# Two-layer hybrid decoder on one core: sparse attention heads on two row halves of TensorE, the fifth step's state-space block behind the value products, compression on two column groups

## The chip, the cores and the metric

One core of one Trainium2 chip runs the whole program. The metric is the device time in microseconds (us) of one execution; the kernel before was timed in three runs. TensorE (PE) multiplies, and its weight loads have rows of their own (PEld); VectorE (DVE), ScalarE (ACT) and GpSimd (POOL) do the rest, and SyncE (SP) issues most transfers. Matmul results land in PSUM, here eight banks of 128 x 512 float32.

## The reference, cut to what matters

```python
for l in range(DEPTH):                              # DEPTH = 2, 256 tokens, width 1024
    u = rms_norm(h_res, norm_mix[l]) @ w_in[l]
    y_a = mla_mixer(u...)      # 4 heads, 64+32 wide, causal softmax attention
    y_b = nsa_mixer(u...)      # 4 heads, 64 wide, three branches over shared keys
    y_c = rglru_mixer(u...)    # gated linear recurrence
    y_d = ssd_mixer(u...)      # state-space block, chunks of 128
    h_res = h_res + concat(rms_norm(y_a), rms_norm(y_b), rms_norm(y_c), y_d) @ w_out[l]
    h_res = h_res + (swiglu if l == 0 else moe_ffn)(rms_norm(h_res, norm_ffn[l]))

def nsa_mixer(u, ...):
    # q: 4 heads x 64; keys and values: 3 pairs x 64, shared by the heads
    kc, vc = compress(keys0), compress(vals0)       # 32 x 64 inputs -> 64, for 15 windows of 32 tokens
    o = gate0 * softmax(q kc) vc + gate1 * softmax(q k_sel) v_sel + gate2 * softmax(q k_win) v_win
```

With 256 tokens the selection takes all four blocks of 64 and the window of 512 covers everything, so "sel" and "win" are both plain causal attention with 64-wide heads.

## The kernel before

Everything is written out by hand: each engine has its own program, and counting semaphores tie them together. There are two layers. In each, a mixer (about 90 us) is followed by a feed-forward part, dense after the first mixer and eight experts after the second, in which w_hi/w_lo parts of the weights are multiplied. All of the change lies in the mixers.

The attention part of a mixer is a pipeline of eight jobs, `AJ = mla0, mla1, sel0, sel1, win0, win1, cmp0, cmp1`: a branch and a block of 128 query tokens (0 or 1). Block 0 sees 128 keys and block 1 sees 256; "cmp" sees 15 compressed keys. At step n the engines do, each in the order of its program:

- TensorE: `scores(n)` (four heads, L732), at n = 4 the state-space block `ssd_sums` (L817 to L838), `products(n - 2)` (probabilities times values, L780), `turn_probs(n - 1)` (transposes of the probabilities, L749); and at n = 0 the gates of the recurrence (L812), at n = 2 inside `products(0)` the compression (`compress`, L790), at n = 3 `turn_keys`, at n = 5 `ssd_cb` (L848), at n = 6 `ssd_products`. `keep_busy` (L713) issues matmuls whose result nobody reads.
- VectorE: `score_rows(n)` (mask, scale and row minimum of each head, L2149), at n = 4 the state-space block (L2218 to L2235), at n = 2 the copy of the compressed keys and values (L2240) and a convolution (`conv`, L2087 and L2091), then `outputs(n - 2)` (L2166 to L2190).
- ScalarE: `exps(n)` (L1576 and L1573), then `turned_probs(n - 1)` (copies the transposed probabilities out of PSUM, L1586), and at n = 2 the two Silu calls (L1630 and L1631) between which and the exponentials it reloads its function table; at n = 4 the exponentials of the state-space block (L1637).

TensorE's results for VectorE go to banks 0 to 3 in turn (`bank(0)`), those for ScalarE to banks 4 to 7 (`bank(1)`); `bank` waits until the bank of four uses ago has been read, and `give` signals that a bank is full. `score_rows(n)` waits until ScalarE has copied out the transposed probabilities of job n - 2, since it writes over that job's `prob`; `products(n)` waits for the copy of job n itself.

A 64-wide float32 head occupies rows (partitions) 0 to 63 of its operands, so half of the array's rows. Each float32 matmul shows as two records in the trace, each with a weight load; a transpose shows as one. Before the pipeline the queries are turned by L679 (64 wide, two heads to a bank, two banks, read by ScalarE's L1552), the compression's inputs by L687 and L688, the keys by L693, and the dense-attention queries and keys by L704 (read by L1563).

Of the kernel before, what the change touches and what calls it, by code (L numbers as in the profile page):

```python
# [22 lines left out]
P = 128  # L23
# [17 lines left out]
def trunk(nc, x, positions, norm_mix, w_in, mla_q_norm, mla_w_uq, mla_kv_norm, mla_w_ukv, nsa_cmp_pe,  # L41
# [33 lines left out]
    with ctx:  # L75
# [101 lines left out]
        def at(start, *shape):  # L177
            used[0] = start
            return take(*shape)

        mix_bufs = []
        for l in range(L):
            i0 = (BASE_MIX[l] + 7) % SPLIT
            b1, b2 = (split_at + SLOT * i for i in (i0, SPLIT + i0))
            b3, b4, b5, b6 = (split_at + SLOT * (SPLIT * j + (i0 + i) % SPLIT) for j in range(2) for i in (1, 2))
            mix_bufs.append((
                at(b1, TB, MLA_H, QK), take(TB, MLA_H, QK),
                at(b2, 2, S), take(6, S),
                at(b3, MLA_H, S), take(MLA_H, S),
                at(b4, NH, S), take(2, S), take(NC), take(2 * HD), take(TB, SSD_H), take(4, HD),  # L190
                at(b5, CLEN // 2, 2, NC), take(TB, GW), take(TB, GW), take(SSD_H, P), at(used[0] - SSD_H * P, 2, S),
                at(b6, SSD_H, S)))
# [18 lines left out]
        def probT_cmp(n):  # L211

            return probT[:, n % 2, 7 * P:8 * P] if n == 6 else probT[:, n % 2, 0:P]

        def prob_of(n):
# [88 lines left out]
        left_hi = sem("left_hi")  # L304
        left_lo = sem("left_lo")
        cn_ready = sem("cn_ready")
        qk_roped, nsa_roped, cin_ready, gate_th = sem("qk_roped"), sem("nsa_roped"), sem("cin_ready"), sem("gate_th")
# [92 lines left out]
        def _(pe):  # L400
# [168 lines left out]
            for l in range(L):  # L569
# [102 lines left out]

                pe.wait_ge(nsa_roped, l + 1)
                for hp in range(2):
                    b = bank(1)
                    for i in range(2):
                        c0 = O_NSA + (2 * hp + i) * HD
                        for tb in range(TB):
                            mm = pe.transpose(b[0:HD, (2 * i + tb) * P:(2 * i + tb + 1) * P],  # L679
                                              utok[:, tb, c0:c0 + HD], ident[:, :])  # L680
                    give(mm, 1)
                b = bank(1)
# [32 lines left out]
                def scores(n):  # L715
                    br, tb = AJ[n]
                    t0, t1 = tb * P, (tb + 1) * P
                    nk = NC if br == "cmp" else t1
                    if br == "cmp":
                        pe.wait_ge(dve_took, mark["cmp", l])  # L720
                    per = 4 if br == "cmp" else 512 // nk
                    for g in range(4 // per):
                        b = bank(0)
                        if n == 7:
                            keep_busy(b, 2)
                        for i in range(per):
                            h = g * per + i
                            q, k = {"mla": (qT[0:QK, h, t0:t1], kT[0:QK, h, 0:nk]),
                                    "cmp": (nqT[0:HD, h, t0:t1], kcT[0:HD, :]),
                                    "sel": (nqT[0:HD, h, t0:t1], kswT[0:HD, 0, 0:nk]),  # L730
                                    "win": (nqT[0:HD, h, t0:t1], kswT[0:HD, 1, 0:nk])}[br]
                            mm = pe.matmul(b[:, i * nk:(i + 1) * nk], q, k, start=True, stop=True)  # L732
                        give(mm, 0)
                    mark["scores", l, n] = gave[0]
# [50 lines left out]
                def compress(b):  # L785

                    pe.wait_ge(cin_ready, l + 1)
                    for c in range(2):
                        for j in range(CLEN // 2):
                            mm = pe.matmul(b[0:NC, c * HD:(c + 1) * HD], cin[:, j, c, :], w_cmp[:, j, c * HD:(c + 1) * HD],  # L790
                                           start=(j == 0), stop=(j == CLEN // 2 - 1))
                    give(mm, 0)
                    mark["ckv", l] = given[0]
# [131 lines left out]
                for n in range(len(AJ) + 2):  # L925
                    if n < len(AJ):
                        scores(n)
                    if n == 4:
                        ssd_sums()
                    if n >= 2:  # L930
# [3 lines left out]
                    if 1 <= n <= len(AJ):  # L934
                        turn_probs(n - 1)
                    if n == 0:
                        lru_gates()
# [269 lines left out]
        def _(pool):  # L1207
# [63 lines left out]

            for l in range(L):
                roots(1, 0, False)
                roots(1, 1)
# [22 lines left out]
                pool.wait_ge(*filled_by[1][mark["nsa", l] - 1])  # L1297
                pool.memset(utok[:, :, KV0 + 4 * HD:KV0 + 4 * HD + 1], 1.0).then_inc(sum_cols, 1)
                roots(2, 0, False)
                roots(2, 2)  # L1300
# [50 lines left out]
        def _(act):  # L1351
# [127 lines left out]
            for l in range(L):  # L1479
# [69 lines left out]

                for hp in range(2):  # L1550
                    b = filled()
                    act.activation(nqT[0:HD, 2 * hp:2 * hp + 2, :],  # L1552
                                   b[0:HD, :].rearrange("p (h t) -> p h t", h=2), ACT.Copy).then_inc(act_took, 1)
                b = filled()
# [213 lines left out]
        def _(dve):  # L1768
# [203 lines left out]
            for l in range(L):  # L1972
# [163 lines left out]
                def score_rows(n):  # L2136
# [3 lines left out]
                    if n >= 2:  # L2140
                        dve.wait_ge(act_took, mark["probT", l, n - 2])
                    per = 4 if br == "cmp" else 512 // nk
                    scale = float(QK if br == "mla" else HD) ** -0.5
                    m = cmbias[:, tb, :] if br == "cmp" else cbias[:, P - tb * P:2 * P]
                    for g in range(4 // per):
                        b = filled()
                        for i in range(per):
                            h = g * per + i
                            ins = dve.tensor_tensor_reduce(prob_of(n)[:, h, :], b[:, i * nk:(i + 1) * nk], m,  # L2149
                                                           -scale, -NEG, ALU.add, ALU.min, rmin[:, n, h:h + 1])  # L2150
                        empty_bank(ins)
# [57 lines left out]
                for n in range(len(AJ) + 2):  # L2209
# [3 lines left out]
                    if n < len(AJ):  # L2213
                        score_rows(n)
                    if n == 4:

# [17 lines left out]
                        for tb in range(TB):  # L2234
                            step(dve.tensor_tensor(xdt[:, tb, :].rearrange("p (h d) -> p h d", h=SSD_H),  # L2235
                                                   xtok[:, tb, :].rearrange("p (h d) -> p h d", h=SSD_H),
                                                   dts[:, 4, tb, :].unsqueeze(2).broadcast_to([P, SSD_H, HD]), ALU.mult))
                    if n == 2:
                        b = filled()
                        empty_bank(dve.tensor_copy(ckv[0:NC, :], b[0:NC, 0:2 * HD]))  # L2240
                        tell(conv(xbc, xraw, "scw", "scb", 6, 4, 6), "ssd_conv", ssd_conv)
                    if 1 <= n <= len(AJ) and AJ[n - 1][0] == "cmp":
                        mask_cmp(n - 1)
                    if n >= 2 and n != 8:
                        outputs(n - 2)

                    if n == 0:
# [406 lines left out]
```

## Time and profile before

| | us |
|---|---|
| Median of 3 runs (1509.17 to 1509.39) | 1509.21 |
| The profiled execution, its own time | 1509.64 |
| Its span in the trace | 1507.9 |
| Attention pipeline of layer 0, first scores to first output projection | 80.6 to 122.5 |
| The same of layer 1 | 457.8 to 499.8 |

Busy time counts the time in which an engine has an instruction in flight. TensorE's matmuls overlap and their ends are modelled, so for TensorE the starts are read: the distance between the starts of two groups is what the first took. The idle time before a group stands in square brackets with what ended it. The second layer's mixer repeats the first's nearly to the hundredth, 377.2 us later.

### The profile page before, as it was taken

What the parts mean: (1) busy time and instruction counts of PE and PEld (TensorE: products, weight loads), DVE (VectorE), ACT (ScalarE), POOL (GpSimd) and SP (SyncE); (2) the same over time, 40 slices, a digit from 0 to 9 for tenths busy, and PEclk for the clock granted to TensorE, in tenths of its full rate; (3) what the DMA queues carried; (4) which work ended last, traced back from release to release, by engine and by line L of the source; (5) the groups of instructions that cost most, each with busy time, mean ns of one, the idle gap of its engine ahead of it and who ended that gap; (6) DMA issues with size and microseconds to landing.
All of it is one profiled execution on the core that took longest, in us unless ns stands there. A gap on an engine that the chain in (4) does not pass through costs nothing.

```text
span 1507.9 us, 20053 instructions
## 1 busy us (share of the span) xinstructions
PE 1486.9 (99%) x7413; PEld 1245.8 (83%) x7413; DVE 1213.4 (80%) x1283; ACT 1000.3 (66%) x894; POOL 82.7 (5%) x126
## 2 busy tenths in 40 slices
PE   9999999999999999999999999999999999999997
PEld 7987888888898888888888888888888888888885
DVE  7778545545577899989898899898988899889986
ACT  7376543444547577787777777777777777778765
POOL 3102000000000110000000000000000000000000
PEclk9999999999999999999999999999999999999999
DMA  9705655555530379999999999999999999999992
GB/s 319 249 2 131 240 176 195 194 195 170 190 115 2 112 274 396 396 354 394 395 346 394 394 356 384 394 380 357 396 394 345 394 396 342 395 396 344 393 396 87
DMA packets 189980, 444.23 MB, mean 295 GB/s; under 512 B 9729, under 2 KB 16014, under 8 KB 189918
## 3 DMA queue, kind: packets, MB, share of 16 engines
q1 hardware_dynamic: 185366, 427.81, 77.5%
q0 software_dynamic: 4528, 15.58, 3.9%
q8 instruction: 39, 0.64, 0.2%
q14 instruction: 23, 0.19, 0.0%
q10 hardware_dynamic: 24, 0.01, 0.0%
HBM read 435.51 MB, written 7.86 MB: 294 GB/s over the span
## 4 chain that ended last, share of the span: by engine, by line
PE 94%; DVE 2%; ACT 2%; issue 1%; POOL 0%; SPq 0%; DMA 0%; POOLq 0%; DVEq 0%; ACTq 0%
PE bank L478 27%; PE bank L479 27%; PE bank L477 27%; PE bank L618 3%; PE bank L540 2%; PE bank L732 1%; PE bank L621 1%; PE bank L780 1%; PE bank L749 1%; PE bank L790 0%; PE bank L1020 0%; DMA ring<-in_w_in_dram 0%; POOL rstd L1303 0%; PE bank L650 0%; PE bank L713 0%
## 5 line engine op out<-in xcount | busy, mean ns | idle before, releaser
L1909 DVE TENSOR_TENSOR w_lo<-ring,w_hi 128x2048 fp32r<-128x2048 f32 x372 | 846.4, 2290 | 176.1 <-ACT w_hi L1427 175.6
L1427 ACT ACTIVATE w_hi<-ring 128x2048 fp32r<-128x2048 f32 x372 | 712.2, 1917 | 221.7 <-PE bank L477 221.7
L478 PE MATMUL bank<-w_hi,xT_hi 128*128 128x512 f32 x896 | 353.5, 395 | 0.0
L479 PE MATMUL bank<-w_hi,xT_lo 128*128 128x512 f32 x896 | 349.4, 390 | 0.0
L477 PE MATMUL bank<-w_lo,xT_hi 128*128 128x512 f32 x896 | 240.2, 390 | 0.0
L478 PE MATMUL bank<-w_hi,hidT_hi 128*128 128x512 f32 x560 | 220.6, 394 | 0.0
L479 PE MATMUL bank<-w_hi,hidT_lo 128*128 128x512 f32 x560 | 218.2, 390 | 0.0
L477 PEld LDWEIGHTS bank<-w_lo,xT_hi 128*128 128x128 f32 x896 | 168.1, 188 | 36.0 <-DVE w_lo L1909 0.3
L479 PEld LDWEIGHTS bank<-w_hi,xT_lo 128*128 128x128 f32 x896 | 168.3, 188 | 33.9
L478 PEld LDWEIGHTS bank<-w_hi,xT_hi 128*128 128x128 f32 x896 | 168.3, 188 | 33.6
L478 PE MATMUL bank<-w_hi,hT_hi 128*128 128x512 f32 (+2 forms) x384 | 147.3, 387 | 4.8 <-DVE hT_lo L1864 2.7
L477 PE MATMUL bank<-w_lo,hidT_hi 128*128 128x512 f32 x560 | 149.4, 389 | 0.0
L479 PE MATMUL bank<-w_hi,hT_lo 128*128 128x512 f32 (+2 forms) x384 | 145.2, 381 | 0.0
L477 PEld LDWEIGHTS bank<-w_lo,hidT_hi 128*128 128x128 f32 x560 | 105.1, 188 | 22.2
L479 PEld LDWEIGHTS bank<-w_hi,hidT_lo 128*128 128x128 f32 x560 | 105.2, 188 | 21.2
L478 PEld LDWEIGHTS bank<-w_hi,hidT_hi 128*128 128x128 f32 x560 | 105.2, 188 | 21.2
L1433 ACT ACTIVATE hidT_hi<-bank 128x512 fp32r<-128x512 f32 x68 | 40.1, 599 | 92.5 <-PE bank L540 92.5
L1887 DVE TENSOR_TENSOR w_lo<-ring,w_hi 128x2048 fp32r<-128x2048 f32 (+1 forms) x34 | 77.1, 2280 | 24.6 <-ACT w_hi L1392 23.2
L477 PE MATMUL bank<-w_lo,hT_hi 128*128 128x512 f32 (+2 forms) x384 | 92.6, 381 | 0.5 <-DVE w_lo L1887 0.5
L478 PEld LDWEIGHTS bank<-w_hi,hT_hi 128*128 128x128 f32 x384 | 72.6, 189 | 20.3 <-issue 3.1
L479 PEld LDWEIGHTS bank<-w_hi,hT_lo 128*128 128x128 f32 x384 | 72.5, 189 | 13.1
L1392 ACT ACTIVATE w_hi<-ring 128x2048 fp32r<-128x2048 f32 (+1 forms) x33 | 62.5, 1904 | 30.9 <-PE bank L477 15.3
(393 smaller groups left out, 1269.6 us busy)
## 6 DMA issues: line engine op xcount, KB each, us to landing
ring<-in_moe_w_gate_dram SPq DMA_DIRECT2D x112, 1024.0 KB, 9.4
ring<-in_moe_w_up_dram SPq DMA_DIRECT2D x112, 1024.0 KB, 9.4
ring<-in_moe_w_down_dram SPq DMA_DIRECT2D x112, 1024.0 KB, 9.1
ring<-in_ffn_w_gate_dram SPq DMA_DIRECT2D x14, 1024.0 KB, 5.2
ring<-in_ffn_w_up_dram SPq DMA_DIRECT2D x14, 1024.0 KB, 5.1
ring<-in_ffn_w_down_dram SPq DMA_DIRECT2D x14, 1024.0 KB, 4.8
ring<-in_w_in_dram SPq DMA_DIRECT2D x11, 1024.0 KB, 5.3
ring<-in_w_out_dram SPq DMA_DIRECT2D x8, 1024.0 KB, 8.9
```

The costliest lines, as they stand in the source:

```text
L477: return pe.matmul(o, x_hi, w, start=False, stop=stop)
L478: pe.matmul(o, x_hi, w, start=start, stop=False)
L479: return pe.matmul(o, x_lo, w, start=False, stop=False)
L540: mm = pe.transpose(banks[2 + v][:, f * P:(f + 1) * P], hid[:, v, f * P:(f + 1) * P], ident[:, :])
L618: mm = pe.matmul(b[i][:, 0:S], wk, hT_hi[:, 4 * h + k, :], start=start and not low, stop=stop and low)
L621: pe.matmul(b[i][:, 0:S], wk, hT_lo[:, 4 * h + k, :], start=False, stop=False)
L732: mm = pe.matmul(b[:, i * nk:(i + 1) * nk], q, k, start=True, stop=True)
L1392: act.activation(dst[:, :, 0:n], slot_k(p)[:, :, 0:n], ACT.Copy).then_inc(hi_ready, 1)
L1427: act.activation(w_hi[:, (base + at) % SPLIT, :], ring[:, i, :], ACT.Copy).then_inc(hi_ready, 1)
L1433: act.activation(hidT_hi[:, v, :], banks[2 + v][:, :], ACT.Copy).then_inc(hidT_hi_ready, 1)
L1887: dve.tensor_tensor(dst[:, :, 0:n], slot_k(p)[:, :, 0:n], hi[:, :, 0:n], ALU.subtract)\
L1909: dve.tensor_tensor(w_lo[:, v, :], ring[:, (base + at) % RING, :], w_hi[:, v, :].bitcast(F32), ALU.subtract).then_inc(lo_ready, 1)
```

## The change

The queries' four 64-wide heads are turned two at a time, so that heads 0 and 2 lie in partitions 0 to 63 and heads 1 and 3 in 64 to 127. GpSimd copies the keys (`kswT`, 64 x 512 float32) and later the compressed keys (`kcT`) to the upper partitions with two transfers per layer. The scores of sel, win and cmp alternate between the two row halves, each half with its own bank; so block 0 now takes two banks where it took one. The dense attention (mla) gets the same interleaving of two banks in block 1, without row halves. The compression alternates between its two operands, the second one's output at partitions 32 to 46. The state-space block of step 4 moves behind `products` and `turn_probs` on TensorE, and behind `outputs` on VectorE.

```diff
-                at(b4, NH, S), take(2, S), take(NC), ...
+                at(b4, NH // 2, S), take(2, S), take(NC), ...
+        def heads_of(n):
+            br, tb = AJ[n]
+            if br == "mla":
+                return [[0, 1, 2, 3]] if tb == 0 else [[0, 1], [2, 3]]
+            return [[0, 2], [1, 3]]
...
                 pe.wait_ge(nsa_roped, l + 1)
+                b = bank(1)
                 for hp in range(2):
-                    b = bank(1)
-                    for i in range(2):
-                        c0 = O_NSA + (2 * hp + i) * HD
-                        for tb in range(TB):
-                            mm = pe.transpose(b[0:HD, (2 * i + tb) * P:(2 * i + tb + 1) * P],
-                                              utok[:, tb, c0:c0 + HD], ident[:, :])
-                    give(mm, 1)
+                    c0 = O_NSA + 2 * hp * HD
+                    for tb in range(TB):
+                        mm = pe.transpose(b[:, (2 * hp + tb) * P:(2 * hp + tb + 1) * P],
+                                          utok[:, tb, c0:c0 + 2 * HD], ident[:, :])
+                give(mm, 1)
...
                     if br == "cmp":
                         pe.wait_ge(dve_took, mark["cmp", l])
-                    per = 4 if br == "cmp" else 512 // nk
-                    for g in range(4 // per):
-                        b = bank(0)
-                        if n == 7:
-                            keep_busy(b, 2)
-                        for i in range(per):
-                            h = g * per + i
-                            q, k = {"mla": (qT[0:QK, h, t0:t1], kT[0:QK, h, 0:nk]),
-                                    "cmp": (nqT[0:HD, h, t0:t1], kcT[0:HD, :]),
-                                    "sel": (nqT[0:HD, h, t0:t1], kswT[0:HD, 0, 0:nk]),
-                                    "win": (nqT[0:HD, h, t0:t1], kswT[0:HD, 1, 0:nk])}[br]
+                        pe.wait_ge(keys_in, 32 * (l + 1))
+                    elif br == "sel":
+                        pe.wait_ge(keys_in, 32 * l + 16)
+                    groups = heads_of(n)
+                    held = [bank(0) for _ in groups]
+                    if n == 7:
+                        keep_busy(held[0], 2)
+                    for i in range(len(groups[0])):
+                        for b, heads in zip(held, groups):
+                            h = heads[i]
+                            r = slice(h % 2 * HD, (h % 2 + 1) * HD)
+                            nq = nqT[r, h // 2, t0:t1]
+                            q, k = {"mla": (qT[0:QK, h, t0:t1], kT[0:QK, h, 0:nk]), "cmp": (nq, kcT[r, :]),
+                                    "sel": (nq, kswT[r, 0, 0:nk]), "win": (nq, kswT[r, 1, 0:nk])}[br]
                             mm = pe.matmul(b[:, i * nk:(i + 1) * nk], q, k, start=True, stop=True)
-                        give(mm, 0)
+                            if i == len(heads) - 1:
+                                give(mm, 0)
...
-                    for c in range(2):
-                        for j in range(CLEN // 2):
-                            mm = pe.matmul(b[0:NC, c * HD:(c + 1) * HD], cin[:, j, c, :], w_cmp[:, j, c * HD:(c + 1) * HD],
-                                           start=(j == 0), stop=(j == CLEN // 2 - 1))
+                    for j in range(CLEN // 2):
+                        for c in range(2):
+                            mm = pe.matmul(b[32 * c:32 * c + NC, c * HD:(c + 1) * HD], cin[:, j, c, :],
+                                           w_cmp[:, j, c * HD:(c + 1) * HD], start=(j == 0), stop=(j == CLEN // 2 - 1))
...
                         scores(n)
-                    if n == 4:
-                        ssd_sums()
                     if n >= 2:
                         products(n - 2)
...
                         turn_probs(n - 1)
+                    if n == 4:
+                        ssd_sums()
...
+                pool.wait_ge(act_took, mark["nsa", l])
+                pool.dma_start(kswT[HD:P, :, :], kswT[0:HD, :, :]).then_inc(keys_in, 16)
+                pool.wait_ge(dve_took, mark["cmp", l])
+                pool.dma_start(kcT[HD:P, :], kcT[0:HD, :]).then_inc(keys_in, 16)
                 roots(2, 0, False)
...
-                for hp in range(2):
-                    b = filled()
-                    act.activation(nqT[0:HD, 2 * hp:2 * hp + 2, :],
-                                   b[0:HD, :].rearrange("p (h t) -> p h t", h=2), ACT.Copy).then_inc(act_took, 1)
+                b = filled()
+                act.activation(nqT[:, :, :], b[:, :].rearrange("p (h t) -> p h t", h=2), ACT.Copy)\
+                    .then_inc(act_took, 1)
...
+                    if n == 2:
+                        b = filled()
+                        dve.tensor_copy(ckv[0:NC, 0:HD], b[0:NC, 0:HD])
+                        empty_bank(dve.tensor_copy(ckv[0:NC, HD:2 * HD], b[32:32 + NC, HD:2 * HD]))
+                        tell(conv(xbc, xraw, "scw", "scb", 6, 4, 6), "ssd_conv", ssd_conv)
+                    if 1 <= n <= len(AJ) and AJ[n - 1][0] == "cmp":
+                        mask_cmp(n - 1)
+                    if n >= 2 and n != 8:
+                        outputs(n - 2)
                     if n == 4:
...
```

VectorE's `score_rows` follows the new grouping of heads; its step-2 copy, `mask_cmp` and `outputs`, which stood behind the block of step 4, now stand ahead of it, and nothing else of them changes but the second copy.

## Rows read from the trace of the kernel before

**Rows 1.** The page, busy time, share of the span and instructions.

```profile
PE 1486.9 (99%) x7413; PEld 1245.8 (83%) x7413; DVE 1213.4 (80%) x1283; ACT 1000.3 (66%) x894; POOL 82.7 (5%) x126
```

**Rows 2.** Timeline of TensorE, layer 0: start, duration, line, shapes, count, [idle before].

```profile
80.58 1.16 PE L732 MATMUL bank<-work 96*128 96x128 f32 x8 [0.86 <-ACT work L1563]
...
83.31 1.89 PE L732 MATMUL bank<-work 96*128 96x256 f32 x8
...
85.57 1.16 PE L732 MATMUL bank<-work 64*128 64x128 f32 x8
86.65 3.75 PE L790 MATMUL bank<-w_cmp,work 128*15 128x64 f32 x64
...
92.24 1.99 PE L732 MATMUL bank<-work 64*128 64x256 f32 x8
...
98.02 0.66 PE L823 MATMUL bank<-ident,work 128*128 128x128 f32 x4
...
101.07 0.49 PE L836 MATMUL bank<-upper,work 128*128 128x128 f32 x2 [0.39 <-DVE work L2149]
...
102.51 1.00 PE L780 MATMUL bank<-work 128*128 128x65 f32 x8
...
104.32 1.99 PE L732 MATMUL bank<-work 64*128 64x256 f32 x8
...
109.92 1.06 PE L732 MATMUL bank<-work 64*128 64x15 f32 x8
```

**Rows 3.** Timeline of TensorE, layer 1.

```profile
478.29 0.49 PE L836 MATMUL bank<-upper,work 128*128 128x128 f32 x2 [0.38 <-DVE work L2149]
```

**Rows 4.** Timeline of ScalarE, layer 0.

```profile
86.05 1.71 ACT L1576 ACTIVATE work<-work 128x256 f32<-128x256 f32 x4 [0.58 <-DVE work L2149]
...
91.91 1.08 ACT L1586 ACTIVATE work<-bank 128x512 f32<-128x512 f32 x2 [0.95 <-PE bank L749]
93.02 1.28 ACT L1630 ACT_TABLE_LOAD   x1
...
97.63 1.71 ACT L1576 ACTIVATE work<-work 128x256 f32<-128x256 f32 x4
99.24 0.57 ACT L1586 ACTIVATE work<-bank 128x512 f32<-128x512 f32 x1
...
105.98 1.04 ACT L1637 ACTIVATE work<-work 128x1024 f32<-128x1024 f32 x1
```

**Rows 5.** Timeline of VectorE, layer 0.

```profile
84.50 0.42 DVE L2149 CUSTOM_DVE_ANT_0 work<-bank,cbias 128x256 f32<-128x256 f32 x1
...
90.44 0.28 DVE L2240 COPY work<-bank 15x128 f32<-15x128 f32 x1 [1.24 <-PE bank L790]
...
104.33 0.75 DVE L2235 TENSOR_TENSOR work<-work 128x256 f32<-128x256 f32 x2
...
119.40 0.18 DVE L2166 RECIPROCAL work<-bank 128x4 f32<-128x4 f32 x1 [1.07 <-PE bank L780]
```

**Rows 6.** Timeline of TensorE, where outputs change partitions (L687 and L688).

```profile
74.13 1.03 PE L679 MATMUL bank<-ident,work 128*64 128x128 f32 x8
75.00 0.27 PE L687 MATMUL bank<-ident,work 128*64 128x128 f32 x1
75.20 0.43 PE L688 MATMUL bank<-ident,work 128*64 128x128 f32 x2
75.56 0.30 PE L687 MATMUL bank<-ident,work 128*64 128x128 f32 x1
```

**Rows 7.** Transfers from GpSimd's queue: count, KB each, us to landing.

```profile
normed_rows<-hn POOLq DMA_DIRECT2D x2, 512.0 KB, 3.1
...
pos_i<-in_positions_dram POOLq DMA_DIRECT2D x1, 1.0 KB, 6.2
```

**Rows 8.** TensorE's last matmul; then stretches: length, busy times, PEclk, DMA.

```profile
1499.22 0.40 PE L1090 MATMUL bank<-xT_lo,last_pick 128*128 128x512 f32 x1
...
1502.40:1507.90 5.50, 0.00 (x0) 0.00 (x0) 2.08 (x3) 0.00 (x0) 0.99 (x1) 0.50 0.50 192
```

More of the change, by code:

```diff
@@ L189, in trunk @@
                 at(b3, MLA_H, S), take(MLA_H, S),
-                at(b4, NH, S), take(2, S), take(NC), take(2 * HD), take(TB, SSD_H), take(4, HD),
+                at(b4, NH // 2, S), take(2, S), take(NC), take(2 * HD), take(TB, SSD_H), take(4, HD),
                 at(b5, CLEN // 2, 2, NC), take(TB, GW), take(TB, GW), take(SSD_H, P), at(used[0] - SSD_H * P, 2, S),
@@ L305, in trunk @@
         left_lo = sem("left_lo")
+        keys_in = sem("keys_in")
         cn_ready = sem("cn_ready")
@@ L1272, in _ @@
             for l in range(L):
+                (qtok, kcat, xb, xbc, qT, kT, nqT, kswT, kcT, ckv, nacs, cvals, cin, xtok, xdt, dec1, kvT2,
+                 dec0) = mix_bufs[l]
                 roots(1, 0, False)
@@ L2141, in score_rows @@
                         dve.wait_ge(act_took, mark["probT", l, n - 2])
-                    per = 4 if br == "cmp" else 512 // nk
                     scale = float(QK if br == "mla" else HD) ** -0.5
                     m = cmbias[:, tb, :] if br == "cmp" else cbias[:, P - tb * P:2 * P]
-                    for g in range(4 // per):
+                    for heads in heads_of(n):
                         b = filled()
-                        for i in range(per):
-                            h = g * per + i
+                        for i, h in enumerate(heads):
                             ins = dve.tensor_tensor_reduce(prob_of(n)[:, h, :], b[:, i * nk:(i + 1) * nk], m,
@@ L2237, in _ @@
                                                    dts[:, 4, tb, :].unsqueeze(2).broadcast_to([P, SSD_H, HD]), ALU.mult))
[L2238 to L2245, printed above, removed]
                     if n == 0:
```

## The prediction

> **What bounds the kernel now.** I read the page first: TensorE has something in flight for 99% of the span [rows 1], so any work taken from it could count. That share can't be spent as it stands, because the change touches only two mixers, and in them the four engines hand one job to each other. So I read the timelines of TensorE, ScalarE and VectorE over one attention pipeline side by side. TensorE hardly waits: 0.86 us before the first scores, for ScalarE's copies, and 0.39 us inside the state-space block, for a bank that VectorE has not read [rows 2]. Layer 1 shows the same 0.38 us at the same place [rows 3]; I work out layer 0 and count it twice. What matters is how close the other engines follow. ScalarE finishes copying job 2's transposed probabilities at 99.24 + 0.57 = 99.81 [rows 4], and TensorE first wants them in `products(2)` at 102.51 [rows 2]. That 2.7 us of slack exists because the state-space block (98.02 to 102.51) stands ahead of `products(2)`. The change takes this block away from there.
>
> **Part by part, TensorE.** Times are for layer 0.
>
> *Query transposes.* Eight 64-wide transposes from 74.13 [rows 6] take 0.87 us to the next group, so 0.11 each; four 128-wide ones remain: 0.44 us less. The first scores wait for ScalarE's copies (0.86 us, rows 2), and ScalarE, one copy shorter too, gets its banks 0.44 us earlier, so scores(0) starts 0.44 earlier.
>
> *Dense attention, block 1.* The two banks are now filled alternately, so the first is full after three heads and not two. A 256-column record takes 0.21 us (1.89 for eight, less the last one's tail, rows 2), a head 0.43. That cancels the 0.44: VectorE starts its rows at about 84.38 and not at 84.50 [rows 5], and ScalarE's exps(1) at 85.93 and not 86.05 [rows 4].
>
> *Row halves.* No row shows two matmuls of one size side by side, so this price is bounded: nothing gained, up to a full overlap of neighbours. Each head is two records on the same rows, which must follow each other, so of eight slots five remain at best: 3/8 less. For 256 columns that is 3 x 0.21 = 0.64 us, in scores(3) and scores(5). For 128 columns (1.08 us from 85.57 to 86.65) and 15 columns (1.06) the record spacing is the same 0.11 though the columns are eightfold fewer [rows 2]: there the weight load sets the pace, and no row shows two loads at once. I take the gain for 256 columns, nothing for 15, and keep 0 and 0.3 us as ends for those.
>
> *Compression.* 64 records in 86.65 to 90.33 are 3.68 us. Alternating partners on different output columns: between no gain and half, 1.8 us. I take 1.8: at 0.057 a record the stream, not the weight load (15 columns), seems to set it.
>
> *A cost below nothing.* Where outputs change partitions today, the next load starts 0.20 us after the last matmul, and one transpose with the pair behind it takes 75.00 to 75.56, 0.56 us for three records against 0.33 without a change [rows 6]. But this is also a change between a transpose and a matmul in a part of the array. The Trainium skill (TensorEngine Tiling, Tiling Modes, Key Properties) says that changing the mode drains the engine while changing the tile within a mode does not, and that tiles load and multiply in parallel; by it the 128- and 15-column scores gain too. Both readings are rivals below, priced from rows.
>
> *The transfers.* Each layer issues two more from GpSimd's queue. That queue holds nothing else then but memsets ahead and the roots behind, which wait for step 4 anyway. `kswT` is ready about 78.1; landing took 3.1 us for 512 KB and 6.2 at worst for a small one [rows 7]: with 0.7 us to issue, 81.9 to 85.0, wanted at about 85.1. `kcT` has over 10 us. Hidden, the first narrowly at the worst price.
>
> **The order around step 4.** ScalarE's program from exps(1) on is full: 85.93 + 1.6 + 0.5 for job 0's copy, 1.6 for the recurrence, 1.3 for exps(2) reach 90.9. It no longer waits 0.95 us for TensorE's transposes, which come earlier. From 91.91 (job 1's copy) to 99.81 (end of job 2's copy) it is 7.9 us of copies, two table loads, Silu and exponentials [rows 4] with no wait longer than 0.1; started at 90.9, it ends at 98.8. The convolution that Silu needs starts when VectorE is through with rows(2), about 1.2 us earlier than 90.44 [rows 5], less 0.15 for the second copy; it is in time.
>
> TensorE is through with scores(4) at about 95.9: 98.02, less 0.44, 1.8 and 0.64, plus 0.7 it must wait at `products(1)` for ScalarE's copy of job 1. There it now meets `products(2)` and waits until 98.8, **2.9 us**. From there: products(2) and turn_probs(3) 104.32 - 102.51 = 1.81; the block 102.51 - 98.02 less the 0.39 wait = 4.10; so scores(5) begins at 98.8 + 5.9 = 104.7, 0.4 later than before (104.32, rows 2), and ends 0.25 earlier with its 0.64. That is the heart of it: 2.9 us taken from TensorE ahead of step 4 and the 0.39 wait buy a stall, since the longer pole up to there is ScalarE. The Trainium skill (TensorEngine Tiling, Performance Considerations, PSUM Bottleneck) warns that tiling does not speed up the emptying of PSUM; the rows of ScalarE agree.
>
> VectorE's half of the block now waits for TensorE's, which runs from 100.6 to 104.7. Its last piece (104.33 + 0.75 = 105.1 before, rows 5) ends near 106.8, and ScalarE's 1.5 us of block exponentials start near 106.2 (105.98 before, rows 4). Carried on with the same durations, job 4's copy is there at 110.35 and TensorE wants it at 110.65: hidden by 0.3 us. After that TensorE sets the end again: VectorE waits 1.07 us for products(5) before 119.40 [rows 5]. So 0.25 us earlier stays: **0.5 us for both layers**. The span falls to 1507.4, its execution from 1509.64 to 1509.1; against the median 1509.21 that is 1508.7.
>
> **The rivals.**
>
> - *Weight loads overlap too.* Scores(6) and (7) lose 0.3 us each behind the stall: 0.25 + 0.6 = 0.85 per layer, 1507.5. For it the rule above; against it nothing in the rows. No clear change either.
> - *No or half an overlap.* Without any, TensorE would be ready at 97.6, ScalarE at 99.4 (it again waits for transposes, 0.44 earlier): scores(5) begins at 105.3, 0.95 late per layer: 1511.1. With only the compression faster, 0.4 late: 1510.0.
> - *The other side, slower: each change of tile costs like a change of mode.* A pair in the compression takes 0.2 us and not 0.11: 32 x 0.1 = 3.1 us; three changes in each score group at 0.2: 0.6 us, six groups. The stall vanishes, and TensorE is later by 3.1 + 3.6 less 0.44 and 0.39, about 5.8 us per layer: 1520.8. It decides from about 0.05 us a change on. For it 75.00 to 75.56 [rows 6], against it that those are mixed kinds.
> - *Slower by the clock.* The granted clock stands at 0.50 from 1502.40, 2.8 us after TensorE's last matmul (1499.22 + 0.40) [rows 8]; a 2.9 us wait in mid-pipeline could do the same. At half speed the next 5 us of TensorE's work cost about 2.5: 1511.2 for one layer, 1513.7 for both.
> - *Faster: the savings survive.* If ScalarE's pole were not there, 0.44 + 1.8 + 2 x 0.64 + 0.39 + some 0.9 of small scores would stay, 4.8 us per layer: 1499.6. For it the 99% [rows 1]; against it ScalarE's rows, in which I find no idle time to remove.
>
> **How the numbers follow.** A change of 0.2%, 3.0 us, is about what a measurement of this kernel can tell from none. Chances: the forecast 0.34; loads overlap too 0.22; none or half 0.20; tile changes 0.06; the clock 0.08, half of it in both layers; the savings survive, whole or over 3 us, 0.10. Faster: the last, with a little of the second, 0.12. Slower: tile changes, the clock twice, and some 0.04 of late transfers or a longer block on VectorE, 0.14. Same: 0.74. The range reaches from below the second case (1507.5, less 1 for what I may have mis-sized) to the clock lost once: 1506.5 to 1511.8.
>
> **What would show it.** After the change, TensorE waits 2 to 3 us before `products(2)`, released by ScalarE's copy of job 2, near 98.8. Groups of 256-column scores take 1.1 to 1.3 us instead of 1.9, the compression 1.9 instead of 3.7; those of 15 columns keep 1.0. The wait inside the block is gone. The granted clock stays 1.00. The prediction is wrong if `products(2)` starts well before 98, if a release by a transfer stands before scores(2), or if alternating groups take longer than before.

## The result and the profile after

The changed kernel takes 1513.98 us (median of 10 runs, 1511.66 to 1515.84) against 1509.24 (10 runs, 1508.99 to 1509.44): a ratio of 1.003, 95% interval 1.0021 to 1.0038. It is slower by 0.3%, and outside my range. The profiled execution took 1514.92 us, with a span of 1513.2, and TensorE's granted clock was 0.992 on average. One execution of experiment 3 below (2151 us, mean clock 0.65) was in a far slower state of unknown cause and is left out of every figure.

The page's busy times, against [rows 1]:

```profile
PE 1482.2 (98%) x7405; PEld 1241.7 (82%) x7405; DVE 1213.8 (80%) x1285; ACT 999.8 (66%) x892; POOL 84.9 (6%) x130
```

TensorE is busy for 4.7 us less, and yet the span is 5.3 us longer. The timeline of TensorE in layer 0 (start, duration, line, shapes, count, idle before), against [rows 2]:

```profile
80.13 1.16 PE L742 MATMUL bank<-work 96*128 96x128 f32 x8 [0.86 <-ACT work L1579]
...
85.11 0.71 PE L742 MATMUL bank<-work 64*128 64x128 f32 x8
86.08 1.97 PE L801 MATMUL bank<-w_cmp,work 128*15 128x64 f32 x64 [0.25 <-DVE work L2163]
...
90.01 1.14 PE L742 MATMUL bank<-work 64*128 64x256 f32 x8
91.88 1.97 PE L791 MATMUL bank<-work 128*128 128x65 f32 x16 [0.73 <-ACT work L1602]
...
94.61 0.72 PE L742 MATMUL bank<-work 64*128 64x128 f32 x8
98.69 1.94 PE L791 MATMUL bank<-work 128*128 128x65 f32 x8 [3.36 <-ACT work L1602]
100.42 1.91 PE L760 MATMUL bank<-ident,work 128*128 128x128 f32 x8
...
108.68 1.14 PE L742 MATMUL bank<-work 64*128 64x256 f32 x8
...
113.43 0.62 PE L742 MATMUL bank<-work 64*128 64x15 f32 x8
114.59 1.08 PE L791 MATMUL bank<-work 128*128 128x65 f32 x8 [0.54 <-DVE work L2305]
115.50 1.04 PE L760 MATMUL bank<-ident,work 128*128 128x128 f32 x8
...
125.74 0.47 PE L486 MATMUL bank<-w_hi,hT_hi 128*128 128x512 f32 x1
```

Every local saving is there, and for the scores more than forecast: the 64-row groups of 256, 128 and 15 columns went from 1.99, 1.16 and 1.06 us to 1.14, 0.71 and 0.62, the compression from 3.75 to 1.97. The stall stands where it was forecast, before `products(2)` (L791), at 98.69 and released by ScalarE's copy (L1602). But the eight records behind it take 1.73 us to the next group, where the same eight of a later job take 0.91 (114.59 to 115.50). That is the reading that matters: the same instruction is twice as slow behind the stall. The stretches say why (length, busy times, granted clock as PEclk, DMA share, GB/s):

```profile
80.00:95.00 15.00, 13.84 (x153) 12.05 (x155) 11.90 (x57) 13.20 (x27) 0.00 (x0) 1.00 0.01 3
95.00:100.00 5.00, 1.64 (x13) 1.48 (x11) 3.71 (x14) 3.87 (x9) 0.52 (x1) 0.75 0.01 1
100.00:105.00 5.00, 5.00 (x25) 5.00 (x26) 1.63 (x5) 3.02 (x10) 0.92 (x2) 0.50 0.00 0
105.00:110.00 5.00, 5.00 (x32) 4.50 (x32) 2.60 (x8) 0.00 (x0) 0.04 (x1) 0.73 0.00 0
475.00:480.00 5.00, 1.64 (x17) 1.41 (x16) 4.09 (x15) 3.99 (x8) 0.52 (x1) 0.98 0.01 1
480.00:485.00 5.00, 5.00 (x33) 5.00 (x33) 1.67 (x7) 3.38 (x10) 0.96 (x2) 0.68 0.00 0
535.00:540.00 5.00, 4.55 (x23) 3.74 (x23) 3.63 (x21) 4.67 (x5) 2.76 (x5) 0.78 0.66 253
```

The clock has two levels, 2.4 GHz (1.00) and 1.2 GHz (0.50), so a mean of 0.75 over 5 us is 2.5 us at half speed. Layer 0 was at half speed for 2.5 + 5.0 + 2.7 = 10.2 us, from within the stall (97.5) on. Layer 1, whose stall is equally long, was at half speed for only 3.4 us, and there the fall came at 479.8, 0.6 us after the stall had ended. A third such stretch of 3.4 us lies in the router, from 537.8 on. Before the change all stretches up to TensorE's last matmul stand at 1.00. The same stall in layer 1; the eight records behind it take 1.19 us and not 1.73:

```profile
479.17 1.40 PE L791 MATMUL bank<-work 128*128 128x65 f32 x8 [3.36 <-ACT work L1602]
```

ScalarE's timeline shows what the stall waits for, and what the late block of step 4 costs further on, against [rows 4]:

```profile
96.36 1.70 ACT L1592 ACTIVATE work<-work 128x256 f32<-128x256 f32 x4
97.97 0.57 ACT L1602 ACTIVATE work<-bank 128x512 f32<-128x512 f32 x1
...
110.22 1.06 ACT L1653 ACTIVATE work<-work 128x1024 f32<-128x1024 f32 x1 [6.31 <-DVE work L2254]
```

The copy of job 2 ends at 98.54 (forecast 98.8). The block's exponentials start at 110.22, where 106.2 was forecast. With the clock held (experiment 1) they start at 105.89, so the half-speed stretch made them 4.3 us late. The two transfers, from the view of DMA issues (KB, us to landing), against [rows 7]:

```profile
work<-work POOLq DMA_DIRECT2D x1, 128.0 KB, 2.3
work<-work POOLq DMA_DIRECT2D x1, 3.8 KB, 1.6
```

The first was issued at 78.44 in 0.61 us, so it lands near 81.4 (78.44 + 0.61 + 2.3) for a need at 85.11: hidden, as forecast.

### The profile page after: what moved, and what is told of

Same layout as the page of the kernel before. It is cut to its first block, busy times and chain, and to the rows that moved or that the text cites. A ratio compares the mean times of both kernels' runs of the same rounds, so it can differ in the third digit from the quotient of the medians.

```text
span 1513.2 us, 20055 instructions
## 1 busy us (share of the span) xinstructions
PE 1482.2 (98%) x7405; PEld 1241.7 (82%) x7405; DVE 1213.8 (80%) x1285; ACT 999.8 (66%) x892; POOL 84.9 (6%) x130
## 4 chain that ended last, share of the span: by engine, by line
PE 92%; ACT 3%; DVE 2%; issue 1%; POOL 0%; SPq 0%; DMA 0%; POOLq 0%; DVEq 0%; ACTq 0%
PE bank L486 27%; PE bank L487 27%; PE bank L485 27%; PE bank L626 3%; PE bank L548 2%; PE bank L629 1%; PE bank L791 1%; ACT work L1592 1%; PE bank L742 0%; PE bank L1031 0%; PE bank L760 0%; POOL rstd L1320 0%; DMA ring<-in_w_in_dram 0%; PE bank L658 0%; PE bank L720 0%
```

## The experiments

All twelve ran five rounds beside the kernel before (medians 1509.31, 1509.47 and 1509.39 us in the three sets). The kernel before is not quite steady itself: 6 of its 79 executions there took 1510.7 to 1511.3 us at a mean clock of 0.997, where the rest show 0.998 or 0.999, so it too seems to lose the clock now and then; no trace of such an execution was kept. Theory 1: the savings are there, and the clock that falls in the stall before `products(2)` takes them and more. Its rival, theory 2: the new place of the state-space block costs the time, since VectorE's and ScalarE's halves come late, and the clock is an accompaniment. The first expectation numbers its cases by itself: its theory 2 is that the paired matmuls bring the clock down, its theory 3 that the wait alone is the loss. "A fall" is the granted clock going from 1.00 to 0.50.

**1. The stall filled with work.** Six matmuls nobody reads (12 records) are issued ahead of the waiting `products(2)`; nothing else changes.

```diff
                    if n == 6:
                        keep_busy(b, 3)
+                    if n == 2:
+                        keep_busy(b, 6)
```

> The changed kernel with 12 records of matmuls nobody reads (6 calls, about 2.6 us) just ahead of products(2)'s wait of 3.36 us. Theory 1 (the idle wait makes the clock fall, and that is the loss): the granted clock stays 1.00 through both mixers, products(2) still starts near 98.7, and the time falls to 1507 to 1508.5, a little below the kernel before. Theory 2 (the row halves and column groups themselves let the clock fall, since fewer records are in flight): the clock still falls, 1512 to 1516. Theory 3 (the wait itself is the loss, the clock adds little): 1512 to 1514 with the clock at 1.00.

Measured: 1507.52 us (1507.3 to 1507.8), ratio 0.9988 [0.9979, 0.9997], clock 0.998. TensorE's timeline, and two of the stretches:

```profile
95.28 2.86 PE L720 MATMUL bank<-cbias,ident 128*128 128x256 f32 x12
98.62 1.11 PE L793 MATMUL bank<-work 128*128 128x65 f32 x8 [0.48 <-ACT work L1604]
...
104.32 1.13 PE L742 MATMUL bank<-work 64*128 64x256 f32 x8
...
110.27 1.08 PE L793 MATMUL bank<-work 128*128 128x65 f32 x8 [0.58 <-ACT work L1604]
...
121.42 0.47 PE L486 MATMUL bank<-w_hi,hT_hi 128*128 128x512 f32 x1
```

```profile
95.00:100.00 5.00, 4.52 (x32) 3.73 (x29) 3.94 (x16) 3.87 (x9) 0.52 (x1) 1.00 0.01 1
100.00:105.00 5.00, 5.00 (x46) 4.83 (x46) 3.16 (x10) 2.81 (x10) 0.96 (x2) 1.00 0.00 0
```

`products(2)` begins at the same time (98.62 against 98.69); only the clock differs. The first output projection comes at 121.42 and not 125.74, 4.32 us earlier. Layer 1's comes at 497.51 and not 503.59, so layer 1 itself took 1.76 us more in the changed kernel; the rest of the difference of the two spans (1513.2 - 1505.5 = 7.7 us), 1.6, lies behind it, nearly all in the router. Over the medians the falls cost 1513.98 - 1507.52 = 6.5 us. Theory 1 holds. The paired matmuls are all still in this kernel, and the clock stays at 1.00, so they are not the cause; and `products(2)` starts no earlier, so the wait alone is not either.

**2. Less of the stall filled.** As 1, with 2 in place of 6.

```diff
+                    if n == 2:
+                        keep_busy(b, 2)
```

> The changed kernel with only 4 filler records (0.85 us) ahead of products(2), which leaves about 2.5 us of the wait idle. If what counts is how long TensorE stands idle: the clock still falls in most executions (it fell with 2.8 us idle, and with 1.9 in one layer of two), 1509 to 1512. If any break of the wait is enough: 1507.5 with the clock at 1.00.

Measured: 1512.37 us (1507.91 to 1515.5), 1.0016 [1.0007, 1.0026], clock 0.995.

```profile
98.36 1.47 PE L793 MATMUL bank<-work 128*128 128x65 f32 x8 [2.21 <-ACT work L1604]
```

With 2.21 us left idle the clock still fell in both layers of the profiled execution, and only one execution of eleven (1507.91, clock 0.998) came near experiment 1; the median is 1.6 us below the changed kernel's. Filling a part of the stall leaves most of the loss.

**3. The new order alone.** The kernel before, with the block of step 4 moved on TensorE and VectorE as in the change; one row half, old compression.

```diff
                        scores(n)
-                    if n == 4:
-                        ssd_sums()
                     if n >= 2:
                         products(n - 2)
...
                         turn_probs(n - 1)
+                    if n == 4:
+                        ssd_sums()
```

> The kernel before with only the order of step 4 changed (block behind products and turn_probs on TensorE, behind outputs on VectorE); no row halves, no column groups. Theory 1: products(2) waits about 1.8 us for ScalarE's copy at 99.8, the 0.39 us wait in the block goes, scores(5) begins near 105.7 against 104.3: 2.5 to 3 us slower in all, 1511 to 1512.5, with the clock at 1.00 since the wait is short. Rival (the order is harmless, only the shortened work ahead makes the wait): 1508.5 to 1509.5.

Measured: 1516.89 us (median of five, 1515.39 to 1521.11), 1.0056 [1.0043, 1.0069]. The timelines of layer 0 and layer 1:

```profile
99.72 1.08 PE L780 MATMUL bank<-work 128*128 128x65 f32 x8 [1.87 <-ACT work L1586]
...
478.25 1.94 PE L780 MATMUL bank<-work 128*128 128x65 f32 x8 [1.87 <-ACT work L1586]
```

I had expected the clock to stay at 1.00. Two stalls of the same 1.87 us in one execution: behind the first the clock stays, behind the second it is at half (0.72 from 475 to 480, 0.50 from 480 to 485). So a shorter stall than the changed kernel's is enough, not always.

**4. The new order alone, filled.** As 3, with four matmuls ahead of `products(2)`.

```diff
+                    if n == 2:
+                        keep_busy(b, 4)
```

> The kernel before with the new order alone and 8 records nobody reads (1.7 us) ahead of products(2), whose wait was 1.87 us. Theory 1: the clock stays 1.00, and what is left is the lateness alone, about 1.3 us a layer: 1511.5 to 1512.3. If the order's loss is not the clock: 1515 to 1518 as without the filler.

Measured: 1511.92 us (1511.7 to 1512.51), 1.0017 [1.0008, 1.0026], clock 0.999; the first output projection at 123.60 against 122.5 before. So of the 7.6 us by which experiment 3 (1516.89) is slower than the kernel before (1509.31), the order itself takes some 2.5 (1.1 to 1.2 per layer) and the clock the other 5.0 (1516.89 - 1511.92). Theory 2 has a small part, shown here only for the kernel without row halves.

**5. The old order, the rest of the change kept.** The cut shows TensorE's program; VectorE's block goes back ahead of `outputs` too.

```diff
+                    if n == 4:
+                        ssd_sums()
                     if n >= 2:
                         products(n - 2)
...
-                    if n == 4:
-                        ssd_sums()
```

> The changed kernel with the state-space block back ahead of products and outputs of step 4, as before the change; row halves and column groups stay. Theory 1: the block's first 1.1 us run, then its first decay bank waits for VectorE's rows(4), which wait for the same copy of job 2: about 2.9 us idle until 99.2, so the clock can still fall. Without a fall scores(5) begins near 103.7 against 108.7: 1505 to 1507; with falls as in the changed kernel up to 1511. If the order was the whole of the loss (rival): no wait over 1 us there and 1501 to 1504.

Measured: 1510.68 us (1509.16 to 1511.24), 1.0007 [0.9998, 1.0016].

```profile
99.24 0.80 PE L847 MATMUL bank<-upper,work 128*128 128x128 f32 x2 [2.76 <-DVE work L2163]
```

The stall is not bound to the new order. With TensorE's work ahead of step 4 shortened, the block meets a wait too: for a bank that VectorE frees when it has read scores(4), and those rows are late because they wait for ScalarE's copy of job 2. Both layers fell again (0.73 and 0.58, 0.62 and 0.70 in the stretches used above). The interval leaves this kernel neither faster nor slower than before.

**6. ScalarE's copy moved ahead of the exponentials.** The changed kernel, only ScalarE's program altered: it copies job 2's transposed probabilities before `exps(3)`, not behind.

```diff
+                    if n == 3:
+                        turned_probs(2)
                     if n < len(AJ):
                         exps(n)
-                    if n >= 1:
+                    if n >= 1 and n != 3:
                         turned_probs(n - 1)
```

> The changed kernel with ScalarE's copy of job 2 ahead of exps(3) as its only edit, no filler. products(2) begins near 95.8, but turn_probs(3) then waits until exps(3) is done, near 98.4: about 1.7 us idle, which has let the clock fall in some executions. With the clock at 1.00 scores(5) begins near 103.6: 1505.5 to 1506; with falls 1507 to 1510. If the wait before products(2) was only moved and nothing won: 1511 or more.

Measured: 1510.17 us (1506.88 to 1512.24), 1.0004 [0.9995, 1.0013]. TensorE's timeline:

```profile
95.62 1.08 PE L791 MATMUL bank<-work 128*128 128x65 f32 x8 [0.35 <-ACT work L1602]
98.54 1.97 PE L760 MATMUL bank<-ident,work 128*128 128x128 f32 x8 [1.85 <-ACT work L1592]
```

`products(2)` comes 3.1 us earlier; what is late next is `turn_probs(3)`, for `exps(3)`. That 1.85 us stall again let the clock fall in layer 0 (0.77, then 0.50) and not in layer 1 (1.00, 1.00). The executions spread over 5.4 us, and the time goes with the mean clock: 0.997 in the two fastest, 0.993 or 0.994 in the five slowest.

**7. The block put into that gap.** As 6, and TensorE runs `ssd_sums` between `products(2)` and `turn_probs(3)`.

```diff
                     if n >= 2:
                         products(n - 2)
+                    if n == 4:
+                        ssd_sums()
...
                         turn_probs(n - 1)
-                    if n == 4:
-                        ssd_sums()
```

> The changed kernel with ScalarE copying job 2's transposed probabilities out before it makes exps(3) and not behind it, and with TensorE's state-space block between products(2) and turn_probs(3). Theory 1 (the pole is ScalarE's copy): the copy is done near 95.6 and not 98.5, no wait over 1.5 us is left, the clock stays 1.00, scores(5) begins near 102.2: 1503.5 to 1505.5. Rival (the pole is VectorE or the rest of ScalarE's work): the wait comes back at turn_probs(3) or at the block's banks, 1507 or more.

Measured: 1508.27 us (1507.77 to 1509.6), 0.9993 [0.9984, 1.0002].

```profile
98.44 0.56 PE L839 MATMUL bank<-work,upper 128*128 128x4 f32 x2 [1.39 <-DVE work L2165]
```

A miss for the theory that I had put first; the other case that I had named, a wait that comes back at the block's banks, held. A stall of 1.39 us, for a bank that VectorE has to read, was left, and the clock fell in both layers of the profiled execution.

**8. The same, filled.** As 7, with three matmuls at the head of `ssd_sums`.

```diff
                     b = bank(0)
+                    keep_busy(b, 3)
```

> The copy of job 2 ahead of exps(3), the block between products(2) and turn_probs(3), and 6 records of matmuls nobody reads (1.3 us) at the head of the block, in the wait of 1.39 us that was left there. Theory 1 (idle time of TensorE makes the clock fall): the clock stays 1.00 in both mixers, scores(5) begins near 102.7, 1502.5 to 1504.5. Theory 2 (pairs on two halves or groups let it fall): the clock still falls, 1507 or more.

Measured: 1504.64 us (1504.12 to 1505.03), 0.9967 [0.9955, 0.9979], clock 0.999; scores(5) at 103.14, the projection at 120.15. The filling, six spare matmuls in all, gains 1508.27 - 1504.64 = 3.6 us.

**9. Copy first and filled, with the block back in its old place.** Four matmuls at the head of `ssd_sums`, which stands ahead of `products(2)` as before the change; VectorE's block goes back too. The cut shows only where TensorE's block stands.

```diff
                     if n < len(AJ):
                         scores(n)
+                    if n == 4:
+                        ssd_sums()
                     if n >= 2:
                         products(n - 2)
```

> Row halves, column groups and the early copy of job 2, with the block back ahead of products and outputs of step 4 as before the change, and 8 filler records (1.7 us) at its head. Theory: once the copy is early, the first decay bank waits only for VectorE's rows(4) at about 98.3, and products(2) and turn_probs(3) follow the block: scores(5) begins near 103.0, so 1504.3 to 1505.3, as fast as with the block in the middle; the order of the block is then worth little. If the order matters by itself: over 1506.

Measured: 1504.88 us (1504.56 to 1505.15), 0.9968 [0.9956, 0.9981]. Once the copy is early and the wait is filled, the block's place is worth 0.2 us (1504.88 against 1504.64), which the spread of the executions does not tell from nothing.

**10. The compression one operand after the other.** As 1, the compression's loops as before the change, the second output still on its own columns.

```diff
-                    for j in range(CLEN // 2):
-                        for c in range(2):
+                    for c in range(2):
+                        for j in range(CLEN // 2):
```

> The changed kernel with its wait filled, and the compression's two operands one after the other again (64 records, still on two output column groups). The compression takes 3.7 us and not 2.0; the convolution behind it and with it ScalarE's chain come later, by about 0.7 us a layer: 1508.5 to 1509.5. If all of the 1.7 us a layer counts: 1510.5 to 1511; if none: 1507.5.

Measured: 1508.4 us (1508.05 to 1509.21), 0.9993 [0.9984, 1.0002].

```profile
86.02 3.52 PE L803 MATMUL bank<-w_cmp,work 128*15 128x64 f32 x64 [0.25 <-DVE work L2165]
```

3.52 us against 1.97: the saving comes from alternating, not from the columns alone. Of the 1.55 us per layer only 0.44 reach the end ((1508.4 - 1507.52) / 2); the rest goes into the wait for ScalarE.

**11. The heads issued half by half.** As 1, with heads 0 and 2 issued before 1 and 3.

```diff
-                    for i in range(len(groups[0])):
-                        for b, heads in zip(held, groups):
+                    for b, heads in zip(held, groups):
+                        for i in range(len(heads)):
```

> The changed kernel with its wait filled, and the four heads issued half by half (0, 2 on the upper rows, then 1, 3 on the lower) and not in turn. Only the border between the halves can overlap: 256-column groups take 1.7 us and not 1.1, the small ones 0.9 and not 0.6; behind the wait that is about 0.7 us a layer, since job 4's copy hides a part: 1508.4 to 1509.3. If the engine pairs them whatever the order of issue: 1507.5.

Measured: 1507.22 us (1506.6 to 1507.61), 0.9985 [0.9976, 0.9994]; the groups are as short as before:

```profile
85.14 0.72 PE L742 MATMUL bank<-work 64*128 64x128 f32 x8
...
104.06 1.14 PE L742 MATMUL bank<-work 64*128 64x256 f32 x8
```

A miss for my main number; the other case that I had named held. The trace's records start in pairs 13 ns apart, and the last pair carries the "bank is full" signals of both banks, heads 2 and 3. Those two heads end four records apart in the program, so TensorE did not start the records in the order of issue: the even pairs fit partners four records apart. With the partner 32 records away, as in 10, it hardly did.

**12. All of it together.** Experiment 8 with the heads half by half (11).

```diff
                     b = bank(0)
+                    keep_busy(b, 3)
...
-                    for i in range(len(groups[0])):
-                        for b, heads in zip(held, groups):
+                    for b, heads in zip(held, groups):
+                        for i in range(len(heads)):
```

> The fastest kernel so far (copy of job 2 first, block between products(2) and turn_probs(3), 1.3 us of filler) with the heads issued half by half. The engine has paired them in either order, and the first bank of scores(1) is full one head earlier, which took 0.25 us of wait from the compression: 1504.0 to 1504.5 against 1504.6, clock at 1.00.

Measured: **1503.98 us** (1503.95 to 1504.21), 0.9962 [0.9949, 0.9976], clock 0.999: 5.4 us faster than the kernel before and 10.0 faster than the changed one. TensorE's timeline shows `products(2)`, the filling and scores(5), and between them no stall over 0.34 us:

```profile
95.36 1.08 PE L791 MATMUL bank<-work 128*128 128x65 f32 x8 [0.34 <-ACT work L1603]
96.27 1.51 PE L720 MATMUL bank<-cbias,ident 128*128 128x256 f32 x6
...
102.65 1.14 PE L742 MATMUL bank<-work 64*128 64x256 f32 x8
```

## Why the prediction was wrong

**The step that failed** is the line "The granted clock stays 1.00", and behind it the 0.08 given to the clock. The stall was forecast at the right place, with the right releaser and nearly the right end (98.8; 98.69 measured), and the rows of the end of the kernel [rows 8] had shown the clock falling once TensorE stands still. I priced the stall at its length, and the fall, as an exception, at 2.5 us for 5 us at half speed. Measured, it falls in both layers of the profiled execution and once more in the router, costs 4.3 us in layer 0 (10.2 us at half speed), 1.8 in layer 1 and 1.6 in the router, and 6.5 over the medians. The rival's price of 1513.7 for both layers is near the measured 1513.98, in part by luck: its base, 1508.7, was 1.2 us above the 1507.52 that the kernel takes with the clock held, and its 5.0 us for two falls were 1.5 too few. The Trainium skill (TensorE: Matmul & The Clock Gate, HAM oscillation) tells of a kernel in which waits between groups of matmuls bring the clock down each time, so that each group begins at half speed. This trace agrees in part: 0.50 stands behind the stall of layer 0, but in layer 1 the first 0.6 us behind it still ran at 1.00, and of the equal stalls of experiments 3 and 5 only one each had a fall.

**Row halves and small groups.** "Nothing for 15" failed: 1.06 became 0.62, 128 columns 1.16 became 0.71. The term was mis-sized: I took the weight loads for something that does not overlap, and in the trace the loads of a pair start 7 ns apart. For 256 columns I took 0.64 off and got 0.85: the eight records start in four pairs 0.22 us apart, so four slots remain and not five. The Trainium skill (TensorEngine Tiling, Key Properties) says that tiles load and multiply independently and that a change of mode, not of the tile alone, drains the array. The trace agrees that tiles run side by side and that alternating them costs nothing (pairs 0.22 us apart, as single records were); what a change of mode costs no run here singles out.

**Compression**: 1.8 forecast, 1.78 measured. **Transposes and first scores**: 0.44 earlier forecast, 0.45 measured (80.58 to 80.13). **Transfers**: hidden, as forecast. **The wait in the block** is gone, as forecast.

**The rest of the sum.** With the clock held, experiment 1 gives 1507.52: 1.8 us less than before, where the forecast had 0.5 and the rival "weight loads overlap too" 1.7. The pole of ScalarE was right: a stall that takes 3.36 us where 2.9 were forecast, with scores(5) at 104.32 for 104.7. One overlap behind it was not: job 4's copy was to be hidden by 0.3 us, but `products(4)` at 110.27 waits 0.58 us for it. So from scores(5) on, the three groups of scores save 0.85 + 0.44 + 0.44 and the wait takes 0.58, 1.15 us in all; the first output projection came 1.11 earlier (122.53 to 121.42). That the rival's 1.7 fits so well is in part luck, since it had neither this wait nor the full 0.85.

**"The savings survive"** had 1499.6 and 0.10, on the ground that ScalarE's rows hold no idle time to remove. That was the second wrong reading: what was to be had lay not in idle time but in the order. One copy of 0.57 us stood behind 1.7 us of exponentials that nobody on TensorE needed so soon; with it moved and two gaps filled the kernel reaches 1503.98.

**Open.** Why layer 0 stays at half speed for 10.2 us and layer 1, behind an equal stall, for 3.4; why a stall of 1.87 us lets the clock fall in one layer and not in the other; and why it falls a third time in the router of the changed kernel, where the gap before is 0.45 us. No experiment here separates these. The waits of 0.86, 0.73 and 0.48 us in experiment 1 had no fall behind them.

## What to carry to other kernels

Before shortening a busy engine's work, find the pole of the engine that it will meet next; if the saving becomes a wait of TensorE of one to three microseconds in mid-kernel, price it at twice its length or a little more (here waits of 3.36 us in each of two layers cost 6.5 us more through the clock, 1.87 in each 5.0, and 1.39 in each 3.6), look at the granted clock in a stretch behind it, and fill it with matmuls that nobody reads. Better still, see whether the instruction that releases it can be issued earlier on its own engine: here one moved copy and three spare matmuls per layer brought 1504.64 us, and the block's place hardly mattered any more. In this kernel float32 matmuls on two row halves or column groups ran side by side, weight loads too, when they were issued near each other.

## What the runs showed of the hardware that I had not expected

- Float32 matmuls on the two row halves overlap fully, weight loads included, starts 7 to 13 ns apart: 1.99 to 1.14 us for eight records of 256 columns, 1.06 to 0.62 for 15. This holds whether the halves alternate or come two heads at a time (13 ns), so the records are then not started in the order of issue. It hardly holds for 32 records in a row on one column group, followed by 32 on the other (3.52 us against 1.97).
- The granted clock can fall to half in a stall of 1.39, 1.85 or 1.87 us, and two equal stalls of one execution can differ in it; with stalls of 2.2 to 3.4 us it fell in both layers of each profiled execution. The fall can come after TensorE has begun to work again (0.6 us after the stall's end in layer 1 of the changed kernel). Once down it stayed for 3.4 to 10.2 us while TensorE was fully busy.
- Alternating between row halves or column groups costs nothing that can be read, unlike the 0.20 us where transposes and matmuls change partitions [rows 6].
